# Expert outputs as plain scatters into two rows per token, summed on TensorE by the identity

## The reference, cut to what matters

```python
# per layer; alpha = (2*DEPTH)**0.25; t = 1032 tokens, 32 experts, 2 per token
x   = layer_norm(alpha*x + mix, ln1_g, ln1_b)
# hier_moe(x): group by argmax, then top 2 of the 8 experts in that group
gate   = p_grp * top_p / top_p.sum(-1, keepdims=True)
expert = grp[:, None] * EXPERTS_PER_GROUP + top_i
h = silu(xb @ w_gate[e]) * (xb @ w_up[e])        # w_gate, w_up: 1024 x 512
y = h @ w_down[e]                                # w_down: 512 x 1024
y_tok = sum over the token's two experts of gate * y
x   = layer_norm(alpha*x + y_tok, ln2_g, ln2_b)
```

## Time and profile before

| | us |
|---|---|
| median of 3 runs | 2186.19 |
| profiled execution | 2186.38 |
| its span | 2184.3 |
| PE (TensorE) busy | 2028.0 (93%) |
| DVE (VectorE) busy | 693.1 (32%) |
| ACT (ScalarE) busy | 408.3 (19%) |
| POOL (GpSimd) busy | 268.4 (12%) |

### The profile page before, as it was taken

The page is one execution under the profiler, slowest core; times in us unless marked ns, Lnnn a source line. Parts: engine busy times, 40 slices in busy tenths (PEclk is TensorE's granted clock), DMA queues, the critical chain, the costliest instruction groups (busy, mean ns, idle before and its releaser), DMA issues.

```text
span 2184.3 us, 32227 instructions
## 1 busy us (share of the span) xinstructions
PE 2028.0 (93%) x12912; PEld 1207.5 (55%) x12912; DVE 693.1 (32%) x1351; ACT 408.3 (19%) x1048; POOL 268.4 (12%) x246
## 2 busy tenths in 40 slices
PE   8999999999999999999599999999999989989991
PEld 5666655565555665455366666555655546544550
DVE  4512166662111111111483122766611111111114
ACT  2011123301211111111110111233021111111114
POOL 1200000011111111111231000000011111111104
PEclk9999999999999999999799999999999999999996
DMA  6611131348999999999525011412599999999984
GB/s 223 192 31 38 41 128 68 116 156 331 363 374 380 399 374 380 376 373 362 210 93 149 29 39 32 157 58 103 210 354 373 380 383 386 373 378 374 374 333 165
DMA packets 75114, 527.48 MB, mean 241 GB/s; under 512 B 14298, under 2 KB 23386, under 8 KB 50034
## 3 DMA queue, kind: packets, MB, share of 16 engines
q1 hardware_dynamic: 62162, 491.52, 58.6%
q0 software_dynamic: 12800, 33.84, 6.4%
HBM read 485.69 MB, written 54.08 MB: 247 GB/s over the span
## 4 chain that ended last, share of the span: by engine, by line
PE 84%; DMA 6%; DVE 4%; issue 3%; ACT 1%; POOL 0%; SPq 0%; POOLq 0%; DVEq 0%
PE ps L566 19%; PE ps L874 18%; PE ps L919 10%; PE ps L713 9%; PE ps L854 5%; PE ps L547 4%; DMA arena<-in_w_up 3%; PE ps L870 3%; PE ps L843 3%; PE ps L926 3%; PE ps L898 2%; PE ps L913 1%; DMA arena<-in_w_down 1%; PE ps L755 1%; PE ps L655 1%
## 5 line engine op out<-in xcount | busy, mean ns | idle before, releaser
L874 PE MATMUL ps<-arena 128*64 128x256 f32 x1920 | 449.4, 390 | 4.7 <-DMA arena<-in_w_up 4.7
L876 PE MATMUL ps<-arena 128*64 128x256 f32 x1920 | 449.5, 390 | 0.0
L566 PE MATMUL ps<-arena 128*128 128x344 f32 x1440 | 421.1, 453 | 0.0
L874 PEld LDWEIGHTS ps<-arena 128*64 128x64 f32 x1920 | 254.3, 135 | 177.4 <-issue 27.4
L566 PEld LDWEIGHTS ps<-arena 128*128 128x128 f32 x1440 | 272.0, 190 | 142.9 <-issue 3.6
L919 PE MATMUL ps<-arena 128*64 128x512 f32 x480 | 245.9, 660 | 42.8 <-issue 40.0
L876 PEld LDWEIGHTS ps<-arena 128*64 128x64 f32 x1920 | 253.8, 135 | 0.0
L921 PE MATMUL ps<-arena 128*64 128x512 f32 x480 | 246.2, 661 | 0.0
L1897 POOL DMA_INDIRECT ytok<-arena,gidx x64 | 92.8, 1449 | 947.2 <-ACT arena L1199 414.8
L1659 DVE SCALAR_TENSOR_TENSOR arena<-ps,gates,arena 64x256 f32<-64x256 f32 (+1 forms) x128 | 61.0, 476 | 451.7 <-ACT arena L1174 451.7
L713 PE MATMUL ps<-arena 128*128 128x512 f32 x448 | 195.9, 594 | 2.7 <-issue 2.7
(11 more groups left out here) (247 smaller groups left out, 2070.3 us busy)
## 6 DMA issues: line engine op xcount, KB each, us to landing
arena<-in_w_gate SPq DMA_DIRECT2D x64, 2048.0 KB
arena<-in_w_up SPq DMA_DIRECT2D x64, 2048.0 KB
arena<-in_w_down SPq DMA_DIRECT2D x64, 2048.0 KB
arena<-in_w_in SPq DMA_DIRECT2D x36, 512.0 KB, 3.5
arena<-out_y_all SPq DMA_DIRECT2D x16, 512.0 KB, 3.6
xs<-arena SPq DMA_DIRECT2D x16, 512.0 KB, 2.6
ytok<-arena SPq DMA_DIRECT2D x16, 512.0 KB, 3.6
arena<-ytok SPq DMA_DIRECT2D x16, 512.0 KB, 7.2
```

Of the source, the lines that this page charges most:

```text
L566: last = mm(ps[:, 3 * half + ch, 0:CH], wring[:, slot, k * P:(k + 1) * P], xT[:, k, ch * CH:(ch + 1) * CH], start=(k == 0), stop=(k == KD ...
L874: mm(ps[HALF:P, 2 + q, 0:256], xgT[:, slot, k, 0:HALF], wg_half[slot3][q][:, k], start=(k == 0), stop=(k == KD - 1))
L876: last = mm(ps[0:HALF, 2 + q, 0:256], xgT[:, slot, k, 0:HALF], wu_half[slot3][q][:, k], start=(k == 0), stop=(k == KD - 1))
```

## The change

`ytok` now is one table of 2 x 1032 rows, `rows_of`: row t for a token's first choice and row 1032 + t for its second. The index of the second choice has 1032 added (`k * T`), and `x1_out` writes both halves, so that gathers read the same table and `xs1` is not used. Every row is read by one expert and written back by the same one, so the scatter is a plain one: no add in the DMA, and no wait for the scatter before it. `xg` has four buffers, because the gathered rows are needed once more: VectorE alone takes the output out of PSUM and adds the gathered row to it where the row is a first choice (`first_row` is 1 there and 0 elsewhere). ScalarE copies no output any more; `y_a` is gone, and `y_q` is raised by VectorE.

At the layer's end SyncE loads both rows of each tile (18 loads for 9), and TensorE adds them in PSUM with four products per tile with the identity (`outputs_summed`). Statistics and `shifted2` read PSUM. Between the layers the sums are mixed with transposes and first projections and use a ring of two bank pairs; at the very end they use four. The three weight tiles of the next layer are loaded before the last scatters are waited for.

```diff
@@ x1_out (SyncE)
-                    for dst in (a["xs1"], a["ytok"][0]):
-                        sp.dma_start(dst[ds(b * P, rows), :], x1[0:rows, slot]).then_inc(s[f"x1_out{slot}"], 16)
+                    for k in range(2):
+                        sp.dma_start(rows_of[ds(k * T + b * P, rows), :], x1[0:rows, slot]
+                                     ).then_inc(s[f"x1_out{slot}"], 16)
...
@@ layer end (SyncE)
                 for t in range(NT):
-                    sp.dma_start(xin[t][0:tile_rows(t)], a["ytok"][0, t * P:t * P + tile_rows(t), :]
-                                 ).then_inc(s[f"l2_in{t}"], 16)
...
+                    first_in(t)
+                    second_in(t)
...
@@ TensorE
+            def outputs_summed(l, t):
+
+                rows = P if t < NB else NS
+                ring = 4 if l == DEPTH - 1 else 2
+                pe.wait_ge(s[f"l2_in{t}"], BASE + rows_in(l, t) + 32)
+                if t >= ring:
+                    pe.wait_ge(s["l2_used"], BASE + NT * l + t - ring + 1)
+                settle(pe, s["pe_passed"])
+                for h in range(2):
+                    cols = slice(h * 512, (h + 1) * 512)
+                    mm(ps[0:rows, 2 * (t % ring) + h, :], ident[0:rows, 0:rows], xin[t][0:rows, cols],
+                       start=True, stop=False)
+                    last = mm(ps[0:rows, 2 * (t % ring) + h, :], ident[0:rows, 0:rows], second[t][0:rows, cols],
+                              start=False, stop=True)
+                last.then_inc(s["l2_mm"], 1)
...
                 for t in range(3):
+                    if l > 0:
+                        outputs_summed(l - 1, t + 2)
                     x_turned(t)
...
+                for t in range(2 if l < DEPTH - 1 else NT):
+                    outputs_summed(l, t)
...
@@ down (TensorE)
-                    pe.wait_ge(s["y_a"], BASE + n)
                     pe.wait_ge(s["y_d"], BASE + n)
...
@@ y_evict (VectorE; ScalarE's is removed)
-                    v.tensor_copy(ys[0:live, slot, 512:DM], ps[P - live:P, 7, :]).then_inc(s["y_d"], 1)
+                    if rows == MID:
+                        for t in range(4):
+                            cols = slice(t * 256, (t + 1) * 256)
+                            last = v.scalar_tensor_tensor(ys[HALF:MID, slot, cols], x[HALF:MID, cols],
+                                                          first_row[HALF:MID, col:col + 1],
+                                                          ps[QUART * t:QUART * (t + 1), 5, 0:256], ALU.mult, ALU.add)
+                        last.then_inc(s["y_q"], 1)
+                    here = first_row[0:live, col:col + 1]
+                    v.scalar_tensor_tensor(ys[0:live, slot, 0:512], x[0:live, 0:512], here, ps[0:live, 6, :],
+                                           ALU.mult, ALU.add)
+                    v.scalar_tensor_tensor(ys[0:live, slot, 512:DM], x[0:live, 512:DM], here, ps[P - live:P, 7, :],
+                                           ALU.mult, ALU.add).then_inc(s["y_d"], 1)
...
@@ scatter (GpSimd)
                     pool.sem_inc(s["ys_free"], 1)
-                    pool.wait_ge(s["y_a"], BASE + n + 1)
                     pool.wait_ge(s["y_d"], BASE + n + 1)
                     settle(pool, s["pool_passed"])
-                    if turn_other is not None:
-                        pool.wait_ge(s[f"sc_out{1 - slot}"], 16 * (NE // 2 * l + turn_other))
-                        settle(pool, s["pool_passed"])
-                    g.indirect_dma_start(out=a["ytok"][0],
+                    g.indirect_dma_start(out=rows_of,
                                          out_offset=bass.IndirectOffsetOnAxis(ap=gidx[0:rows, col:col + 1], axis=0),
-                                         in_=ys[0:rows, slot], in_offset=None, compute_op=ALU.add,
-                                         bounds_check=T - 1, oob_is_err=False).then_inc(s[f"sc_out{slot}"], 16)
+                                         in_=ys[0:rows, slot], in_offset=None,
+                                         bounds_check=2 * T - 1, oob_is_err=False).then_inc(s[f"sc_out{slot}"], 16)
...
@@ second LayerNorm (VectorE; ScalarE's added2 and squared2 read summed(t, r) too)
-                        step.mark(v.bn_stats(stat[r, 6 * h:6 * h + 6], xin[t][r, h * 512:(h + 1) * 512]))
+                        step.mark(v.bn_stats(stat[r, 6 * h:6 * h + 6], summed(t, r)[:, h * 512:(h + 1) * 512]))
...
                     for p in range(1, NT):
+                        shifted2(p - 1, rows_at[p - 1], p - 1)
                         statistics2(p, rows_at[p], p)
-                        shifted2(p - 1, rows_at[p - 1], p - 1)
                         scaled2(p - 1, rows_at[p - 1], p - 1)
```

More of the change, by code:

```diff
@@ L111, in ds @@
             return bass.ds(i, n)
+        rows_of = a["ytok"].rearrange("k t d -> (k t) d")
         ident = sb("ident", [P, P])
@@ L245, in build @@
                             for ws3 in (wg, wu))
-        xg = at(26768, 2, DM)
-        xg_by_row = [xg[:, n].rearrange("t (p k) -> t k p", k=KD) for n in range(2)]
+        xg = [at(26768, DM), at(27792, DM), lnp[:, 0], lnp[:, 1]]
+        xg_by_row = [x.rearrange("t (p k) -> t k p", k=KD) for x in xg]
         xgT = at(16448, 2, KD, P)
@@ L256, in build @@
         hidq_by_row = hidq.rearrange("t (f j) -> t j f", j=2)
-        passed_over = at(14448, 2, DM)
+        passed_over = at(0, 2, DM)
         xin = [at(29552 + 1024 * t, DM) for t in range(NB)] + [at(27496, DM, parts=NS)]
+        second = [at(14448 + 1024 * t, DM) for t in range(4)] + [at(o, DM) for o in (37744, 38768, 39792, 28528)] \
+            + [at(26464, DM, parts=NS)]
         FIRST3 = [(c, ch) for ch in range(NCH) for c in range(3)]
@@ L471, in _ @@
                 down_in(NE - 1, 1, ranked_expert(NE - 1))
+                if l < DEPTH - 1:
+                    sp.wait_ge(s["dn_mm"], BASE + NE * (l + 1) - 1 + 2)
+                    for slot in range(3):
+                        c = (l + 1) * NTILE + slot
+                        w_tile(c, slot, c * NCH)
                 sp.wait_ge(s["rk_done"], BASE + l + 1)
@@ L1187, in ht_evict @@
                     last.then_inc(s["ht_a"], 1)
-                def y_evict(e, slot, rows):
-                    n = NE * l + e
-                    live = P if rows == P else HALF
-                    act.wait_ge(s["dn_mm"], BASE + n + 3)
-                    act.wait_ge(s["ys_free"], BASE + n + 1)
-                    if rows == MID:
-                        for t in range(4):
-                            last = nc.scalar.copy(ys[HALF:MID, slot, t * 256:(t + 1) * 256],
-                                                  ps[QUART * t:QUART * (t + 1), 5, 0:256])
-                        last.then_inc(s["y_q"], 1)
-                    nc.scalar.copy(ys[0:live, slot, 0:512], ps[0:live, 6, :]).then_inc(s["y_a"], 1)
                 def pair(e, turn, first, second, then):
```

134 lines of the change are left out of this document (79 added, 55 removed).

## The result

The changed kernel takes 2198.45 us (median of 5 runs, 2197.36 to 2203.09) against 2188.20 for the kernel before (5 runs). The ratio is 1.0059, interval 1.0047 to 1.0071, so between 10 and 16 us, 0.6%: slower, clear of the spread of the runs. The profiled execution has a span of 2195.3 us, 11.0 more than before.

A forecast was written before the change was run, and what follows sets the result against it. DMA was taken to bound the expert stage, at a busy share of 1.00. Terms -26.0 + 2.2 + 19.9 + 13.6 = +9.7 on 2186.4 us gave 2196 us, with an 8-in-10 range of 2176 to 2222.

The forecast's parts named there:

- Scatters, -13.0 per layer: Expert stage: scatters without the add save 105 ns per row, 13.0 us per layer, -26.0 for both.
- 185 ns of a plain row: Expert stage: assumed DMA cost of a plain scattered row, against 290 ns for one with the add.
- lower end of 164: Expert stage: lowest price considered for a plain scattered row, 164 ns, its bytes' cost in a weight load.
- neighbour row: Profile row of plain x1 writes among weight loads, 184 ns per row, used to price a plain scatter.
- second rival: Expert stage: a plain scatter costs as a gather, 327 ns per row, nothing gained there; 2222 us, chance 0.18.
- Evictions, +1.1 per layer: Expert stage: evictions by VectorE alone cost only at the last down, +1.1 us per layer, +2.2 total.
- Between the layers, +19.9: Last eviction to end of first projections takes 98.0 us against 78.1, with TensorE's sums added.
- steps 3 and 4: Between layers and tail: they fail if TensorE waits between sums, or sums wait for VectorE; +19.9 and +13.6 us.
- Tail, +13.6: Last eviction to end of span takes 57.3 us against 43.6, with nine sums on TensorE.
- third rival: Tail: the clock stays at half, eight sums take 7.0 us instead of 3.5, +28; 2224 us, chance 0.08.
- first rival: Expert stage: busiest DMA engines gain most, 147 ns per row, -46.8 us for both layers; 2175 us, chance 0.22.
- +35.7: Evictions, between the layers and tail: predicted cost in us of everything except the scatters.

The follow-up runs named there:

- experiments 4 and 1: The kernel before with only the scatter's add removed, 2149.09 us; and the changed kernel with the add put back into the scatter, 2230.35 us.
- experiment 5: The changed kernel with evictions split between ScalarE and VectorE as before, residual left out; 2187.81 us, ratio 1.0000 to the kernel before.
- add_again: The changed kernel with the add put back into the scatter's DMA, without the wait between scatters; 2230.35 us, ratio 1.0188 to the kernel before.
- wait_again: The changed kernel, plain scatters, with each scatter again waiting until the one before it has landed; 2202.94 us, ratio 1.0065 to the kernel before.
- split_evict: The changed kernel with ScalarE and VectorE sharing evictions as before, residual left out; 2187.81 us, the same run as experiment 5.
- add_wait: The changed kernel with both the add in the scatter and the wait for the scatter before it; 2230.98 us, ratio 1.0213 to the kernel before.
- one_row_sum: The changed kernel with two products per tile instead of four, a token's second row left out; 2180.44 us, ratio 0.9959 to the kernel before.
- experiment 6: The changed kernel with two products per tile instead of four; 2180.44 us, the same run as one_row_sum.
- before_plain: The kernel before with only the scatter's add removed, so outputs overwrite each other and the residual; 2149.09 us, ratio 0.9833 to the kernel before.
- mixed: The changed kernel with VectorE summing tiles 0, 2, 4, 6 and 8, TensorE the others; 2191.85 us, ratio 1.0028 to the kernel before.

## Why the prediction was right, and where its errors met

The forecast of 2196 us and its sign were right (2198.45), and the sum of the parts was +9.7 for a measured +10.3 between medians (by the ratio's interval up to 16). Its terms were less good. In the profiles the two stages gave -28.9 us (forecast -23.8), the place between the layers +22.2 (+19.9), the tail to the last scaling +14.5 (+13.6), the end +4.5 (nothing) and the rest -1.2 (nothing). With the mean of 18 stages the stages would be at -25.4 and the sum at +14.6. So the sign and the main mechanism were right, and that the sum came within 3 us is in part luck.

**1. Scatters, -13.0 per layer.** The removal of the add is worth 16.5 to 18.3 us per layer (experiments 4 and 1). The step that failed is the 185 ns of a plain row, taken from the plain writes of `x1`. The queue's time fell by 299 engine-us over 1787 scattered rows, 167 ns per row; 167 x 1787 / 16 = 18.7 us, a little more than the stages show. In their own time, a gathered row of before took 0.112 x 80 / 44 = 204 ns; 641 engine-us over 3560 rows are 180 per row in the mean, so a plain scattered row takes some 156 ns, an estimate that gives a gathered row the same 204 in both kernels, and below my lower end of 164. That is half of the 311 with the add. The Trainium skill's rule (DMA: Bandwidth & Descriptors, Rules for kernel authors) is that an accumulating DMA reads its destination and writes it later, and I had read it as two passes over a row, so half without the add; the trace agrees with that better than with my neighbour row. The second rival was wrong: a plain scatter does not cost as a gather does. That the gather's price is of its direction fits, but no run tests it.

**2. Evictions, +1.1 per layer.** They cost 6.4 (experiment 5). At the last `down` there are 1.2 us against 0.3, near the +1.1 predicted; that the pairs hide the rest is the step that failed. I had named 0.1 to 1 us per pair as its price without cover, and 5 us over 16 pairs lies within that, though the waits that the profile shows are few and longer (2 of 4.6 us in sum before the quarter's products). Parts 1 and 2 together were forecast at -11.9 per layer and are -12.7 in the mean of 18 stages: two errors of four to five us each that cancelled.

**3. Between the layers, +19.9.** +22.2 in the profile after, and +19.7 and +19.9 in the two variants with the add (97.8 and 98.0 us where 98.0 was predicted). First statistics came at 16.5 for a sum predicted to end at 17.2; in the two variants with the add they came at 17.2 to 17.5, since their last scatter lands later. What the changed kernel has on top is a fall of the clock. TensorE's timeline there, the eight-row tile's sum, the transposes of a tile and a projection:

```profile
1110.79 1.02 PE L559 MATMUL ps<-arena,ident 8*8 8x512 f32 x2
1111.65 1.02 PE L561 MATMUL ps<-arena,ident 8*8 8x512 f32 x2
1112.51 1.10 PE L559 MATMUL ps<-arena,ident 8*8 8x512 f32 x2
1113.40 1.91 PE L561 MATMUL ps<-arena,ident 8*8 8x512 f32 x2
1115.24 1.97 PE L575 MATMUL ps<-ident,arena 128*128 128x128 f32 x8
1117.00 6.35 PE L587 MATMUL ps<-arena 128*128 128x344 f32 x16
```

and of the same instructions in add_again, from the sum's second half on:

```profile
1139.48 1.02 PE L559 MATMUL ps<-arena,ident 8*8 8x512 f32 x2
1140.34 1.02 PE L561 MATMUL ps<-arena,ident 8*8 8x512 f32 x2
1141.28 1.09 PE L575 MATMUL ps<-ident,arena 128*128 128x128 f32 x8
1142.21 4.79 PE L587 MATMUL ps<-arena 128*128 128x344 f32 x16
```

In the first the clock drops to 0.59 over 1112 to 1119 while TensorE has no gap, during products that use 8 rows of it; that costs 0.9 + 0.9 + 1.6 us. wait_again and split_evict have the same fall at the same products and take 100.5 and 99.7 us; add_again, add_wait and one_row_sum, which has two such products instead of four, have not. I did not try a version that differs in the eight-row sum alone, so its part in the fall is argued, not shown. VectorE was not what sums waited for, and steps 3 and 4 stand (experiment 6).

**4. Tail, +13.6.** +14.5 to the end of the last scaling (53.2 against 38.7; forecast 52.4). The sums ended 1.9 us earlier than forecast and the last tile's way from its sum to the last scaling took 9.3 us for 6.6. The clock was 0.97 from 2146 on, so the third rival fell. As its rule in the Trainium skill says (TensorE: Matmul & The Clock Gate, What's actually happening), activity released the throttle, and the trace agrees at both places.

**The end, taken over from before.** From the last scaling to the end of the span I had taken the 4.9 us of before; the profile after has 9.4, so from the last eviction to the end of the span the change costs 19.0 us where part 4 had 13.6. This is the term that failed there, and it belongs to the change: in the table the six kernels in which no adding DMA runs (after, wait_again, one_row_sum, before_plain, split_evict, mixed) all end with 9.4, and the eight in which one runs, as a scatter or as a load, end with 4.6 to 5.9. Two pairs differ in the scatter's add alone, before and before_plain, add_again and after, and both go from 4.9 to 9.4 without it. In the profile after the last output data move at 2187.5, and no record says what the rest of the span waits for, so the reason stays open.

The first rival gave 147 ns per row and was nearest on the scatter's price; it lost on both sides, since the add gave back 37.9 us of time and not 46.8, and the other parts cost about 49 and not the +35.7 that I had.

## What to carry to other kernels

Taking the add out of a scatter's DMA halved the time of its rows here, but the sum has to be paid somewhere. It went from a stage in which it cost some 17 us per layer to two serial places, where TensorE took 3.43 us per tile, at half the clock for the first, and everything else waited for it. Before moving such work, ask not only which engine is idle at the place where it lands but how long that engine takes for it there, and whether it can be shared: the same sums on VectorE for the first tiles, and on later DMAs for the rest, cost 12 to 15 us less between the layers, and shared by VectorE and TensorE 5 us less in the tail. An issue that waits for data stands in front of everything else in its engine's queue; put it behind the small operations that others wait for. And forecast the end of the span as a part of its own.

## What the runs showed that I had not expected

- The same 4528 products of a stage take 534 to 545 us of TensorE, at a granted clock of 0.98 down to 0.95. In the six stages with the add in the scatter TensorE was idle 10 us longer in the mean than in the 18 of the changed kernel and its variants, and busy 5 us longer.
- Kernels with the same expert stage had it in 555.7 to 564.0 us, so a gain of a few us in one profile's stage means nothing; 18 of them gave a mean that does.
- A DMA that adds into SBUF needed 6 to 15 us from issue to landing for 128 rows, 9.5 in the median of 47.
- The clock fell from full to half in a stretch without a gap, in three of five profiles of the same instructions, at products of eight rows.
- The span goes on for 9.4 us behind the last operation where no adding DMA runs in the kernel, and for 4.6 to 5.9 where one does.
